# A two-layer hybrid backbone on one Trainium2 core: another order of projections, scan and scan readout

## The reference

```python
px = (h_x * (1.0 + ca_x) + sa_x) @ w_in[l]
...
f = lbd + (1.0 - lbd) * jax.nn.sigmoid(zf)           # forget gates, two directions
return _heads(1.0 - f), _heads(jnp.log(f))
b = jnp.cumsum(gc, axis=1)
b_last = b[:, -1]
s_new = jnp.exp(b_last)[..., None] * s + jnp.einsum('blhk,blhv->bhkv', kc * jnp.exp(b_last[:, None] - b), vc)
o_inter = jnp.einsum('blhk,bhkv->blhv', qc * jnp.exp(b), s)
...
y = _rms_norm(o, onorm.reshape(N_HEADS, HEAD_DIM).astype(f32))      # o: both directions summed
y = y.reshape(o.shape[0], o.shape[1], GROUP_WIDTH) * jax.nn.silu(gate.astype(f32))
```

## Time and profile before

| | |
|---|---|
| median of three runs | 2293.49 us (2292.64 to 2295.71) |
| the profiled execution: its time, its span | 2297.91 us, 2295.9 us |
| busy: PE, DVE, ACT, POOL | 90%, 58%, 32%, 35% of the span |
| mean granted TensorE clock | 0.928 of full speed |
| chain that ended last | PE 74%, DVE 11%, issue 5%, POOL 5%, DMA 3% |

### The profile page before, as it was taken

How to read it: one execution, slowest core, us unless ns; L and a number is a source line. 1 busy time by engine, 2 the same in 40 slices (tenths; PEclk the granted TensorE clock), 3 DMA queues, 4 the chain that set the end, 5 groups by cost and what they waited for, 6 DMA issues and landing times.

```text
span 2295.9 us, 30599 instructions
## 1 busy us (share of the span) xinstructions
PE 2062.6 (90%) x11900; PEld 1659.2 (72%) x11900; DVE 1335.4 (58%) x2680; ACT 743.0 (32%) x1412; POOL 811.9 (35%) x620
## 2 busy tenths in 40 slices
PE   5886998989987799999989989799899978999897
PEld 3653887666775588888878867487577766888786
DVE  1014678757667889899952460577766682222345
ACT  2112433416641122222233320242426613333442
POOL 0001644611043333333343330254610155555554
PEclk8998898989998799999999999898889988999898
DMA  7242010010010233333321111111010012223221
GB/s 285 110 166 110 19 38 19 19 70 1 2 56 19 81 122 114 126 129 111 119 102 65 65 55 55 37 38 37 20 69 2 25 50 73 92 92 107 95 101 64
DMA packets 24126, 169.77 MB, mean 74 GB/s; under 512 B 2608, under 2 KB 2608, under 8 KB 4784
## 3 DMA queue, kind: packets, MB, share of 16 engines
q1 hardware_dynamic: 22544, 157.87, 19.2%
q10 hardware_dynamic: 1440, 9.96, 1.2%
HBM read 165.72 MB, written 2.10 MB: 73 GB/s over the span
## 4 chain that ended last, share of the span: by engine, by line
PE 74%; DVE 11%; issue 5%; POOL 5%; DMA 3%; ACT 2%; SPq 0%; POOLq 0%; DVEq 0%; ACTq 0%
PE PS L946 26%; PE PS L904 16%; PE PS L717 8%; PE PS L711 7%; PE PS L846 3%; PE PS L866 3%; DMA WR<-in_weights 3%; PE PS L830 2%; PE PS L751 2%; PE PS L836 1%; POOL W L1728 1%; DVE H L1593 1%; DVE H L1591 1%; PE PS L853 1%; POOL ST L1691 1%
## 5 line engine op out<-in xcount | busy, mean ns | idle before, releaser
L946 PE MATMUL PS<-XH,WS 128*128 128x512 f32 (+1 forms) x2112 | 571.7, 358 | 10.0 <-POOL WS L1765 6.9
L946 PEld LDWEIGHTS PS<-XH,WS 128*128 128x128 f32 x2112 | 378.7, 191 | 68.1 <-issue 9.7
L946 PE MATMUL PS<-XL,WS 128*128 128x512 f32 (+1 forms) x1056 | 376.3, 356 | 0.0
L1765 POOL TENSOR_TENSOR WS<-WR,WS 128x1024 fp32r<-128x1024 f32 x88 | 212.3, 2414 | 362.1 <-ACT WS L1158 362.1
L717 PE MATMUL PS<-WR,X 128*128 128x256 f32 x1248 | 288.7, 392 | 1.4 <-DMA WR<-in_weights 1.4
L717 PEld LDWEIGHTS PS<-WR,X 128*128 128x128 f32 x1248 | 244.8, 198 | 37.6 <-DMA WR<-in_weights 2.8
L1169 ACT ACTIVATE W<-PS,PR 128x768 f32<-128x768 f32 (+1 forms) x88 | 78.0, 886 | 464.9 <-PE PS L946 400.4
L946 PEld LDWEIGHTS PS<-XL,WS 128*128 128x128 f32 x1056 | 201.5, 191 | 28.3
L711 PE MATMUL PS<-X,WR 128*128 128x512 f32 (+1 forms) x576 | 208.9, 522 | 2.3 <-issue 1.4
L1650 DVE SCALAR_TENSOR_TENSOR W<-PS,PR,W 128x511 f32<-128x511 f32 (+1 forms) x132 | 83.0, 657 | 217.4 <-ACT W L1169 217.4
L1245 DVE SCALAR_TENSOR_TENSOR W<-WR,SC,W 128x256 f32<-128x256 f32 x336 | 191.1, 610 | 6.0
(11 more groups left out here) (180 smaller groups left out, 3476.1 us busy)
## 6 DMA issues: line engine op xcount, KB each, us to landing
WR<-in_weights SPq DMA_DIRECT2D x144, 1024.0 KB, 4.8
W<-in_ln_rows ACTq DMA_DIRECT2D x4, 1024.0 KB, 4.6
U<-in_bias ACTq DMA_DIRECT2D x2, 1792.0 KB, 7.5
H<-in_x SPq DMA_DIRECT2D x1, 2048.0 KB, 10.4
WR<-in_weights SPq DMA_DIRECT2D x4, 512.0 KB, 3.5
out_h<-H ACTq DMA_DIRECT2D x4, 512.0 KB, 2.6
H<-in_ctx SPq DMA_DIRECT2D x1, 1024.0 KB, 12.5
PR<-in_params SPq DMA_DIRECT2D x1, 624.0 KB, 3.7
```

What stands on the lines that cost most here:

```text
L946: mm = pe.matmul(PS[u.pos][:, lo:hi], w[:, part, k, :], src[:, k, lo:hi], start=(k == 0 and src is xh3 and part == 0), stop=(k == KT - 1 a ...
L1765: pool.tensor_tensor(ws5[:, u.c % 2, 1], half_slot(u), ws5[:, u.c % 2, 0], ALU.subtract).then_inc(w_low, 1)
```

## The change: what it does

- Modulation slots of layer 0 stand one or two behind each of the ten parts of QC, GC and IC, in place of four behind a slot.
- The forget gates have their context parts first. The own stage ends with the two context parts of FCF; the latent parts of FCF follow as steps -2 and -1 of the scan, and the four parts of FCB at steps 0, 1 and 2. GpSimd waits for the gate part that each unit reads.
- The other parts begin at step 3. After three rotated parts, plain parts (QD, KD, VD) and rotated ones alternate. Two slots are thus in use at a time, and a place of the ring is given by the earliest last use.
- The readout is cut: the factor `onorm` is multiplied into the gate `cg` in the own stage, squares, reductions, scaling and gating are eight pieces behind steps 1 to 8 of attention (for each of the two feature blocks a square, a reduction, a scaling and a gating, in that order: `scan_out`, parts 0 to 7), and the transposes are four chunks (layer 1: two) from step 11 of attention on. TensorE begins attention once the last parts are taken and rotated. The squares have another place in `W`.

```diff
@@ the order of the work, module level @@
-IN_ORDER = (QC, GC, IC, FCF, FCB, QA, KVA, QB, KVB, QD, KD, VD)
-OWN_SLOTS = 5
-def weight_stream():
...
+def slot_parts(l, s):
+    ctx = l + 1 < DEPTH or s not in LATENT_ONLY
+    if s in (FCF, FCB):
+        return [("feat", b, w) for w in (1, 0) for b in range(2)]
...
+def mixer_jobs(l):
+    whole = lambda s: [(("in", l, s, 0), p) for p in slot_parts(l, s)]
+    gate = whole(FCF)
+    own = whole(QC) + whole(GC) + whole(IC)
+    extra = [(("mod", 0, i, 0), ("mod", i, 0)) for i in range(MOD_FIRST, 24)] if l == 0 else []
+    mixed, n = [], len(own)
+    for k, part in enumerate(own):
+        mixed += [part] + extra[k * len(extra) // n:(k + 1) * len(extra) // n]
+    mixed += gate[:2]
+    back = whole(FCB)
+    turned = [p for s in (QA, KVA, QB, KVB) for p in whole(s)]
+    plain = [p for s in (QD, KD, VD) for p in whole(s)]
+    rest = turned[:3]
+    for k in range(len(turned) - 3):
+        rest += [plain[k], turned[k + 3]]
+    rest += plain[len(turned) - 3:]
+    beside = {-2: gate[2:3], -1: gate[3:4], 0: back[:2], 1: back[2:3], 2: back[3:4]}
+    units = 4 * NT
+    first = 3
+    m = units + 1 - first
+    for i in range(m):
+        beside[first + i] = rest[i * len(rest) // m:(i + 1) * len(rest) // m]
+    return mixed, beside
...
 def ring_plan():
-        place = (place + 1) % RING
-        if place == 0 and (kind in ("up", "down") or (kind == "mod" and l > 0)):
-            place = 1
+        free = range(1 if kind in ("up", "down") or (kind == "mod" and l > 0) else 0, RING)
+        place = min(free, key=lambda p: -1 if holder[p] is None else final[STREAM[holder[p]]])
...
-        osq = W[:, 0:1536]
+        osq = W[:, 6656:8192]
@@ chunks of attention @@
+                if SCAN_OUT <= i < SCAN_OUT + (4 if has_ctx(l) else 2):
+                    b, w = (i - SCAN_OUT) % 2, (i - SCAN_OUT) // 2
+                    parts.append((b, "scan", w * NLT, (NLT, NT)[w], "act"))
@@ TensorE: hgrn(l) @@
-                wait_all(pe, (mod_done, own_of[l][-1].after[1]))
+                pe.wait_ge(mod_done, mods_done(l))
+                for i in (-2, -1):
+                    projections(l, beside[l, i])
...
-                pe.wait_ge(ro_out, l + 1)
-                pe.wait_ge(job_act, jobs_of[l][-1].after[0])
...
@@ TensorE: attention(l) @@
-                pe.wait_ge(ro_in, ro_parts(l + 1))
+                pe.wait_ge(job_act, jobs_of[l][-1].after[0])
+                pe.wait_ge(qk_in, rope_end(l))
                 pe.wait_ge(s_new, unit_end(l)[2])
                 pe.wait_ge(o_out, unit_end(l)[1])
+                pe.wait_ge(atd, unit_end(l)[1])
...
+                    elif c.kind == "scan":
+                        pe.wait_ge(ro_out, 2 * l + c.a + 1)
+                        for t in range(c.lo, c.hi):
+                            mm = pe.transpose(tb[:, (t - c.lo) * P:(t - c.lo + 1) * P],
+                                              cz[0][:, c.a, t * P:(t + 1) * P], ident)
@@ ScalarE @@
-                            act.activation(x3[:, 4 + b, lo * P:hi * P], bank(n)[:, 0:(hi - lo) * P],
-                                           ACT.Copy).then_inc(ro_in, 1)
+                        elif c.kind == "scan":
+                            dst = x3[:, 4 + c.a, c.lo * P:c.hi * P]
@@ VectorE: project(l) and hgrn(l) @@
                     if j.is_e:
+                        forget(j)
+                    if j.slot == GC:
                         dve.wait_ge(job_act, j.after[0])
+                        for i in range(2):
+                            g = cg[:, 2 * j.a + i, :]
+                            dve.tensor_tensor(g, g, onorm[:, l, :], ALU.mult)
+            def forget(j):
...
@@ end of a step of hgrn @@
                         if j.rope:
                             rotate(j)
+                        if j.is_e:
+                            forget(j)
+            def scan_out(l, part):
+                nt = tiles(l)
+                n = 2 * nt
+                sq = [osq[:, b * 768:b * 768 + n * HD] for b in range(2)]
+                o = [cz[0][:, b, 0:nt * P] for b in range(2)]
...
@@ VectorE: attention(l), at the end of each step @@
+                    if i >= 1:
+                        scan_out(l, i - 1)
@@ GpSimd: hgrn(l) @@
-                pool.wait_ge(e_in, e_end[l])
+                pool.wait_ge(mod_done, mods_done(l))
...
+                        pool.wait_ge(e_in, 8 * l + 4 * u.d + (2 if u.t < NLT else 0) + u.b + 1)
...
-                pool.wait_ge(ro_sq, l + 1)
+                pool.wait_ge(ro_sq, 2 * (l + 1))
```

More of the change, by code:

```diff
@@ L51, in weight_stream, with uses @@
+def uses():
+    u = [("mod", 0, i, 0) for i in range(MOD_FIRST)]
+    for l in range(DEPTH):
+        own, beside = mixer_jobs(l)
+        u += [key for key, _ in own] + [key for i in sorted(beside) for key, _ in beside[i]]
+        u += [("out", l, n, g) for n in range(2) for g in range(KT // KDN)]
         nxt = list(range(24)) if l + 1 < DEPTH else []
         for j in range(FT):
-            s.append(("up", l, j, 0))
+            u.append(("up", l, j, 0))
             for _ in range(2 if j < 2 else 1):
@@ L76, in ring_plan @@
         count[place] += 1
-        plan.append((place, count[place], last.get(place)))
-        last[place] = n
+        plan.append((place, count[place], holder[place]))
+        holder[place] = n
     return plan
@@ L325, in hybrid_backbone @@
         for l in range(DEPTH):
[L326 to L344, removed]
+            own, late = mixer_jobs(l)
+            for when, (key, part) in [(None, p) for p in own] + [(i, p) for i in sorted(late) for p in late[i]]:
+                j = Job()
+                j.l, j.slot, j.key, j.at = l, key[2], key, when
+                j.kind, j.a, j.b = part
+                j.rope = j.kind == "tok" and j.slot in (QA, KVA, QB, KVB)
+                jobs.append(j)
         n_act = n_rope = n_e = 0
@@ L360, in hybrid_backbone @@
         jobs_of = [[j for j in jobs if j.l == l] for l in range(DEPTH)]
-        own_of = [[j for j in js if j.kind == "mod" or j.slot in IN_ORDER[:OWN_SLOTS]] for js in jobs_of]
-        beside_of = [[j for j in js if j not in own] for js, own in zip(jobs_of, own_of)]
+        own_of = [[j for j in js if j.at is None] for js in jobs_of]
         n_sum = n_mac = 0
@@ L406, in hybrid_backbone @@
         for l in range(DEPTH):
-            n, m = len(units_of[l]) + 1, len(beside_of[l])
-            for i in range(n):
-                beside[l, i] = beside_of[l][i * m // n:(i + 1) * m // n]
+            for i in range(-2, len(units_of[l]) + 1):
+                beside[l, i] = [j for j in jobs_of[l] if j.at == i]
         atts = []
@@ L472, in hybrid_backbone @@
                         c.a.last_chunk = c
-                    else:
+                    elif c.kind == "root":
                         c.a.root_chunk = c
@@ L511, in hybrid_backbone, with rope_end @@
         tiles_before = [sum(tiles(l) for l, _ in res[:m]) for m in range(5)]
-        e_end = [sum(j.is_e for j in jobs if j.l <= l) for l in range(DEPTH)]
         def ga_before(m):
             return sum(4 if has_ctx(l) else 2 for l, _ in res[:m])
-        def ro_parts(n):
-            return sum(4 if has_ctx(l) else 2 for l in range(n))
+        def rope_end(l):
+            return sum(j.rope for j in jobs if j.l <= l)
         def copies_end(l):
@@ L702, in projections @@
                         continue
-                    if j.first:
-                        ws[0] = slot(j.key)
-                    wk = ws[0].rearrange("p (k c) -> p k c", k=KT)
+                    wk = slot(j.key).rearrange("p (k c) -> p k c", k=KT)
                     if j.freed:
```

114 lines of the change are left out of this document (48 added, 66 removed).

## The result

The changed kernel takes 2219.39 us (median of four runs, 2216.07 to 2221.32) against 2294.6 us (2292.64 to 2297.33) for the kernel before in the same comparison. The ratio is 0.967, with a 95% interval from 0.9653 to 0.9687: faster, by 75 us. The forecast was 2208, its range 2175 to 2252.

What follows compares the result with a forecast made beforehand. TensorE, busy for 90% of the span, was taken to bound the kernel. Gains of 55 us in layer 0 and 31 in layer 1, together 86, took the profiled 2297.9 to 2212, median 2208 us; range 2175 to 2252.

Steps and rivals of the forecast that it cites:

- Own stage: Layer 0 before the scan: load waits remain only at three slot changes; stage 105 us, ending at 158 instead of 212.6.
- Start of the scan: TensorE's former 16.1 us standstill in layer 0 is covered by two latent FCF parts, 13.8 us; without cover, 12.
- Steps of layer 0: Scan of layer 0: 250 us of TensorE work plus 27 of losses: 13 early, 14 VectorE excess.
- the pairs: Steps 14 to 23, layer 0: heavy and plain VectorE steps average, 112 us against TensorE's 97.3.
- Steps of layer 1: Scan of layer 1: 205 us of TensorE work plus 19.5 of losses, and 1 at the end.
- VectorE's excess: Layer 1 scan, steps 16 to 22: VectorE 74 us against TensorE's 60.6, costing 13.5 us.
- End of the scan: Gaps of 11.0 and 6.4 us before the first scores go, except some 1 us for the last rotation.
- Attention: Readout pieces covered; transposes add 2.8 and 2.0 us, bias-scaling meetings 2.5 per layer, net of the warmer start.
- (1): Rival: heavy steps hold TensorE as before, engines tied step by step; some 42 us less gain, 2250 us; chance 0.12.
- (2): Rival: TensorE bounds everything; scan losses of 27 and 19.5 shrink to about 5 each, 2172 us; chance 0.08.
- (3): Rival: own stage's cut waits return at the ring, 25 us of wait in place of 11, 2222 us; chance 0.05.
- (4): Rival: short waits keep TensorE at 1.2 GHz in both scans; about 2360 us at a third of the work; chance 0.03.

Runs made afterwards that it cites:

- a1: Changed kernel with layer 0's 16 modulation slots back in four blocks of four behind a slot's last part; 2240.4 us, ratio 0.975.
- a3: Changed kernel with all eight forget-gate parts of each layer in the own stage again, other parts from step 0; 2253.6 us, ratio 0.9803.
- b1: Changed kernel with ScalarE taking the projection part ahead of the exponentials of unit i+2 up to step 3; 2206.7 us, ratio 0.9613.
- c1: Changed kernel with ScalarE taking the projection part ahead of the exponentials at every step; 2208.7 us, ratio 0.9611.
- c2: Changed kernel with ScalarE taking parts first at every step and plain parts behind all rotated ones in both layers; 2203.6 us, ratio 0.9597.
- a2: Changed kernel with all rotated parts first and the plain ones behind them, in both layers; 2226.6 us, ratio 0.9688.
- d1: Changed kernel with ScalarE taking parts first everywhere, bias scaling in eight pieces, plain parts last in layer 1 only; 2184.0 us, ratio 0.9508.
- b3: Changed kernel with parts put in steps by VectorE's work, narrow parts in twos; 2246.4 us, ratio 0.9788.
- a4: Changed kernel with the readout's eight pieces ahead of VectorE's attention and transposes at its steps 0 to 3; 2221.4 us, ratio 0.9671.

## Why the prediction was right, and where it was not

**Own stage.** Forecast waits at three changes of slot, 2.5, 2.7 and 2.3 us, and an end at 158. Measured 2.66, 2.53 and 2.15, and the two latent FCF parts of 13.8 us end at 172.25, so the stage ends at 158.4. a1 shows the mechanism alone. One reading was off without harm: of the 25 us that the blocks cost beyond TensorE's own share, 20.4 were idle time (159.60 less 139.15) and the rest products at the low level.

**Start of the scan.** Forecast as covered: right, and a3 shows its size, which the prediction had as 12 us a layer: 17.4 in layer 0 (34.9 less 17.5) and 15.5 in layer 1. The wait alone is 15.35 us in a3, and TensorE works at the low level behind it. The waits for ScalarE in the first steps were forecast as 3.9 and 3.1 us and measured as 4.53 and 2.25; b1 shows that the order of ScalarE's queue is the cause.

**Steps of layer 0.** Forecast 126.7 + 13 us for steps 0 to 12, 97.3 + 14 for 13 to 22, 26 + 1 for the rest. Measured by the starts of the maps: 139.2 (172.3 to 311.5), 115.4 (to 426.9), 26.2 (to 453.1). The clock in steps 6 to 12 was 0.97, as the prediction wanted (above 0.9). So the pairs do average, as c1 against c2 and a2 show in this layer too, by 9 to 10 us. Of GpSimd's four key products between 355 and 400 us each stretched a VectorE instruction, by 2.15, 1.30, 2.46 and 1.29 us. That is 1.8 on average, which makes a plain step 7.9 us by the prediction's own terms (5.8, 0.3 and 1.8), between its 7.7 and its 8.2.

**Steps of layer 1: the step that failed.** The prediction took 205 us of work, 6 for the first steps and 13.5 for VectorE's excess "in steps 16 to 22", and 1 at the end. Measured are 244.7 us in place of 225.5: TensorE idle for 21.5 us and its work stretched from 205 to 223.2 at a granted clock of 0.90. That is 19 us of gain that did not come: 16 us up to attention in place of 35. The term was worked out as a sum over the steps, and a sum does not see where TensorE has no part. Its term for VectorE's excess was mis-sized: the seven steps 16 to 22 took 81.7 us (1537.1 to 1618.7) in place of 74, and the prediction put nothing at step 10, whose empty place cost 1.67 us and slow work behind it, nor at the wait of 2.15 us ahead of step 16. The term of 6 us for the first steps was some 9: the wait of 5.15 and about 4 of slow work. Of the 21.5 us of idle time 15.0 (5.15, 1.67, 8.19) stand directly behind the three empty steps, one of them beside a QB rotation. b1 takes 3.7 us off the first without filling its step, so that one was ScalarE's queue more than the empty step. c2 and d1 move the heavy rotations away from these steps and the scan is 224.5 and 226.8 us. b3 moves the empty steps away from the heavy rotations too, and the long wait is gone, but with its other neighbours the scan is longer. How much of the 19 us the empty steps alone cost stays open: no kernel kept the order and filled them.

**End of the scan.** 11.0 and 6.4 us went, as forecast, but a4 shows that the move of the pieces into attention is not what did it. What is left is that TensorE begins the scores without waiting for the readout, and in layer 0 the second part ahead of them.

**Attention.** Forecast as 5.3 us longer in layer 0 and 4.5 in layer 1. Measured 149.3 against 148.1 before, and 116.0 against 119.5. The transposes are there; TensorE's wait at the scaling of the bias is 4.77 us in place of 3.87 in layer 0 and 3.10 in place of 4.6 in layer 1, and attention of layer 1 runs at a clock of 1.00, where it had 0.95. So the added 2.5 us a layer were too much. That the warmer start was worth more fits the clock, but no run shows it alone.

**The sum.** The start of attention in layer 0 moved by 57.2 us (forecast 60.3), the start of layer 1 by 56.0 (55), of its attention by 72.1 (90), the end by 76.4 (86). The errors in layer 1's scan, 19 us, and in attention, 12 us the other way, make up 10 of the 11 us of the median together with some 3 at the start of the first attention. So the total came this near in part by luck: 22 us of errors one way met 12 the other.

**The rivals.** (1), that nothing averages, did not hold as a whole, but the tie that it named, ScalarE's copies behind a later unit's exponentials, was there and cost 13 us (b1), and it is what made TensorE wait in a2 and b3. Its price was summed wrong: twice 37 us less the 14 and 13.5 in the sum is 46.5 and not 42, so its time was 2254, just outside the range and not inside. (2) would have needed the scans at about 256 and 211 us; even d1 has 272.7 and 226.8. (3) did not come: three waits of 2.66 us and less at the ring. (4): TensorE's clock was 0.94 and 0.90 in the scans, so it took a share of layer 1's gain and no more.

By the runs that undo one part, the gain of 75 us is 31 for the gates at the scan's start, 18 for the modulation slots, 4 for the alternation and nothing for the place of the readout's pieces. No run undid the rest, 22 us. The stretches between the last part and the first scores are 15.8 us shorter in the two layers (11.0 and 6.4 to 0.79 each), with the transposes now in attention; that TensorE does not wait for the readout any more was not undone by itself, and such shares need not add up.

## What to carry to other kernels

When work is spread beside a pipeline, look at each step for itself: a step without filler beside another engine's heaviest step can cost the whole difference and then the clock (8.19 us and the slow work behind it here), and the best order of one layer was the worse one for the next. An order by hand that looks only at one engine's sum can lose more than it gains (b3, 27 us), since a third engine's queue stands between the two. Where an engine waits for a bank, look at what stands ahead of the copy in the queue of the engine that frees it; two exchanged lines were worth 13 us here. Cut a long instruction of a helper engine where a short one of a busy engine can meet it.

## What the hardware showed unexpectedly

Eight GpSimd instructions of 448 columns take 13.06 us where one of 3584 columns takes 10.05, and the kernel is 10 us faster with them: a VectorE instruction on four columns, 0.15 us by itself, took 6.08 us beside the long one. No two-input instruction of VectorE was stretched among the eight pieces. And in the scan of layer 1 waits of 1.7 to 8.2 us were each followed by work at the lower clock level (maps 3.25 us in place of 1.78 behind three of them), so that the stretching of TensorE's work cost nearly as much as its idle time of 21.5 us: some 18 us, an estimate, 223.2 us of busy time less the 205 that the prediction worked out from rows at full clock. Not every wait is followed so: behind the 2.15 us at 150.52 the narrow part took 3.72 us, its length at full clock.
